# A new step order in the last mixing stage and a step table for the recurrence, in a two-block layer kernel

## The reference

```python
def rwkv7_mixer(...):                  # 16 heads of 64
    ...
    def step(state, inp):
        r_t, w_t, k_t, v_t, kk_t, a_t = inp
        sk = jnp.einsum('bhvk,bhk->bhv', state, kk_t)
        state = state * w_t[:, :, None, :] - sk[..., None] * (kk_t * a_t)[:, :, None, :] + v_t[..., None] * k_t[:, :, None, :]
        return state, jnp.einsum('bhvk,bhk->bhv', state, r_t)
    ...
    y = head_norm(y, LNX_EPS) * lnx_g + lnx_b
    bonus = jnp.sum(rh * kh * r_k, axis=-1, keepdims=True) * vh
    out = jnp.einsum('bsf,fd->bsd', (y + bonus) * jax.nn.silu(g), w_out)

def hgrn2_mixer(u, w_in, lb, out_gain, w_out):   # 8 heads of 128
    proj = u @ w_in
    q, fl, inp, g = jnp.split(proj, ...)
    log_f = jnp.logaddexp(jnp.log(lbf), jnp.log1p(-lbf) + jax.nn.log_sigmoid(fl))
    k = -jnp.expm1(log_f)
    ...  # chunk by chunk, b = cumsum(log_f)
        scores = jnp.einsum('bhtd,bhsd,bhtsd->bhts', qb, kb, decay)   # decay = exp(b_t - b_s), causal
        o = scores @ ib + jnp.einsum('bhtd,bhdv->bhtv', qb * jnp.exp(b), state)
        state = jnp.exp(b_last)[..., None] * state + jnp.einsum('bhsd,bhsv->bhdv', kb * jnp.exp(b_last - b), ib)
    o = o * lax.rsqrt(jnp.mean(o * o, axis=-1, keepdims=True) + EPS) * out_gain
    return (o * jax.nn.silu(g)) @ w_out
```

## Time and profile before

| | |
|---|---|
| median of 3 runs | 4136.17 us (4132.33 to 4144.88) |
| profiled execution | 4131.08 us, span of the core 4129.2 us |
| TensorE / its weight load | busy 90% / 73% of the span |
| VectorE / ScalarE | 49% / 40% |
| mean granted clock of TensorE | 0.919 |
| the recurrence's loop | about 1324 to 1980 us of the span |
| the last mixing stage | about 3270 to 3908 us of the span |

### The profile page before, as it was taken

The page is one execution under the profiler, slowest core; times in us unless marked ns, Lnnn a source line. Parts: engine busy times, 40 slices in busy tenths (PEclk is TensorE's granted clock), DMA queues, the critical chain, the costliest instruction groups (busy, mean ns, idle before and its releaser), DMA issues. The chain is left out here.

```text
span 4129.2 us, 48226 instructions
## 1 busy us (share of the span) xinstructions
PE 3724.6 (90%) x18866; PEld 3028.2 (73%) x18866; DVE 2018.7 (49%) x3934; ACT 1667.9 (40%) x3108; POOL 108.1 (3%) x120
## 2 busy tenths in 40 slices
PE   6999789989985999999797999999789999998799
PEld 5888458768873777777675777777677787877686
DVE  3144342453325667675435455555545455555542
ACT  3222461444422333433225344444432565655430
POOL 0011220000000000000000000000000000000000
PEclk9999899989995777788899999999889999999799
DMA  3332312122221211211411111010122211110221
GB/s 126 117 130 100 135 52 86 50 74 92 93 88 48 55 42 42 52 49 34 163 41 47 37 29 32 27 32 26 42 92 77 77 36 36 37 36 11 98 91 41
DMA packets 219705, 265.61 MB, mean 64 GB/s; under 512 B 62684, under 2 KB 142676, under 8 KB 218456
## 3 DMA queue, kind: packets, MB, share of 16 engines
q1 hardware_dynamic: 219480, 262.53, 19.6%
HBM read 191.95 MB, written 70.52 MB: 64 GB/s over the span
## 5 line engine op out<-in xcount | busy, mean ns | idle before, releaser
L320 PE MATMUL bank<-wh,XH 128*128 128x512 f32 x1344 | 553.3, 412 | 38.2 <-DVE wl L304 19.2
L320 PE MATMUL bank<-wh,XL 128*128 128x512 f32 x1344 | 528.3, 393 | 0.0
L320 PE MATMUL bank<-wl,XH 128*128 128x512 f32 x1344 | 528.3, 393 | 0.0
L2402 PE MATMUL bank<-XH,wh 128*128 128x512 f32 x1040 | 427.1, 411 | 32.1 <-DVE wl L2391 19.8
L2402 PE MATMUL bank<-XH,wl 128*128 128x512 f32 x1040 | 411.6, 396 | 0.0
L2402 PE MATMUL bank<-XL,wh 128*128 128x512 f32 x1040 | 410.3, 395 | 0.0
L320 PEld LDWEIGHTS bank<-wh,XH 128*128 128x128 f32 x1344 | 255.7, 190 | 101.8 <-issue 37.9
L320 PEld LDWEIGHTS bank<-wh,XL 128*128 128x128 f32 x1344 | 255.9, 190 | 60.2 <-issue 10.0
L320 PEld LDWEIGHTS bank<-wl,XH 128*128 128x128 f32 x1344 | 255.3, 190 | 55.2
L320 PE MATMUL bank<-XH,wh 128*128 128x512 f32 x704 | 278.3, 395 | 5.5 <-DVE XL L1512 5.5
L304 DVE TENSOR_TENSOR wl<-raw,wh 128x1024 fp32r<-128x1024 f32 x128 | 156.8, 1239 | 255.3 <-ACT wh L295 254.0
(11 more groups left out here) (406 smaller groups left out, 7187.7 us busy)
## 6 DMA issues: line engine op xcount, KB each, us to landing
sc_zt<-stage SPq DMA_DIRECT2D x88, 256.0 KB, 2.0
raw<-in_att_w_in SPq DMA_DIRECT2D x33, 512.0 KB, 4.2
raw<-in_even_w_in SPq DMA_DIRECT2D x32, 512.0 KB, 5.1
raw<-in_odd_w_in SPq DMA_DIRECT2D x32, 512.0 KB, 4.4
raw<-in_rec_w_in SPq DMA_DIRECT2D x32, 512.0 KB, 4.0
sc_h<-H SPq DMA_DIRECT2D x24, 512.0 KB, 2.6
sc_z<-stage SPq DMA_DIRECT2D x40, 256.0 KB, 2.1
z<-sc_z SPq DMA_DIRECT2D x8, 1024.0 KB, 5.5
```

What stands on the lines that cost most here:

```text
L320: done = e.matmul(out, lhsT, rhs, start=k == 0 and j == 0, stop=k == NK - 1 and j == 2)
L2402: done = e.matmul(bank[:, :], x[:, k, :], y[:, k, ts], start=k == 0 and j == 0, stop=k == NK - 1 and j == 2)
```

## The change

In `hgrn_order` the younger head's part is put before the older head's in each step, and VectorE's gate product becomes an event of its own (`gate`) one step after its tile, sorted to the end of that step. In `rwkv_order` the hand-written branches become the table `PLACED`, indexed by 3n + hop. Read against the old branches it places the same events at the same hops, except for two: the solver rows per hop are 4, 2, 3 (the last four in hop 15) in place of 3, 3, 3 (the last one in hop 16), and `gates` stands in hop 6, behind `pack` 1 and `load` of hop 5, in place of ahead of them. The attention stage is the same in both.

```diff
+PLACED = {
+    0: ((1, 'rh'), (1, 'alike', 1), (-1, 'tail', 1, 0)),
+    1: ((-1, 'tail', 1, 1),),
+    2: ((1, 'alike', 2), (1, 'rkr'), (-1, 'tail', 1, 2)),
+    3: ((1, 'alike', 3),),
+    4: ((1, 'pack', 0), (-1, 'tail', 1, 3)),
+    5: ((-1, 'tail', 1, 4), (-1, 'tail', 1, 5), (1, 'pack', 1), (1, 'bonus'), (2, 'load')),
+    6: ((1, 'solve', 4), (0, 'gates')),
+    7: ((1, 'solve', 2),),
+    8: ((2, 'lora', 0), (1, 'solve', 3)),
+    9: ((1, 'solve', 4),),
+    10: ((1, 'solve', 2),),
+    11: ((2, 'lora', 1), (2, 'scan'), (1, 'solve', 3), (0, 'tail', 0, 0)),
+    12: ((1, 'solve', 4),),
+    13: ((0, 'tail', 0, 1), (1, 'solve', 2)),
+    14: ((2, 'norm'), (0, 'tail', 0, 2), (1, 'solve', 3)),
+    15: ((1, 'solve', 4),),
+    16: ((0, 'tail', 0, 3),),
+    17: ((1, 'unpack'), (2, 'spread'), (2, 'centre')),
+    18: ((2, 'unit'),),
+    19: ((2, 'key'), (2, 'exps')),
+    20: ((0, 'tail', 0, 4),),
+    21: ((2, 'be'), (2, 'al')),
+    22: ((2, 'ka'), (0, 'tail', 0, 5)),
+    23: ((2, 'values'), (2, 'alike', 0)),
+}
...
-        some(p + 1, *[("solve", s) for s in solved(n, 0)])
...
-        elif n == 1:
-            if p:
-                order += [("tail", p - 1, 1, 4), ("tail", p - 1, 1, 5), ("gates", p)]
-            some(p + 1, ("pack", 1), "bonus")
-            some(p + 2, "load")
...
+            for q, what, *rest in PLACED[3 * n + j]:
+                if what == "solve":
+                    solve(p + q, rest[0])
+                elif not (what == "gates" and p == 0):
+                    some(p + q, (what, *rest))
...
@@ -2890,18 +2863,22 @@
     for t in range(11 * 7 + 22):
         h, s = min(t // 11, 7), t - 11 * min(t // 11, 7)
+        if s < 22:
+            put(t, "part", h, s)
         if h:
             put(t, "part", h - 1, s + 11)
-        if s < 22:
-            put(t, "part", h, s)
...
             if s == at:
                 tile(t, x, name, half)
+                if name == "g":
+                    put(t + 1, "gate", x, half)
...
+    for t in steps:
+        steps[t].sort(key=lambda x: x[0] == "gate")
...
-            elif what == "tile" and rest[0] == "g":
-                g = self.half(self.buf["g"][x], rest[1])
-                e.wait_ge(*self.copied.at(h, "g", rest[1]))
-                e.tensor_tensor(g, c.banks[self.mms[h, "g", rest[1]]][:, :], g, ALU.mult).then_inc(*self.gated.up(h, rest[1]))
+            elif what == "gate":
+                g = self.half(self.buf["g"][x], rest[0])
+                e.wait_ge(*self.copied.at(h, "g", rest[0]))
+                e.tensor_tensor(g, c.banks[self.mms[h, "g", rest[0]]][:, :], g, ALU.mult).then_inc(*self.gated.up(h, rest[0]))
```

More of the change, by code:

```diff
@@ L1615, in rwkv_order, with solve @@
     steps = [(p, n) for p in range(8) for n in range(NS)]
+    row = {}
     def some(q, *names):
-        if q < 8:
+        if 0 <= q < 8:
             order.extend((x[0], q, *x[1:]) if isinstance(x, tuple) else (x, q) for x in names)
+    def solve(q, rows):
+        for _ in range(rows):
+            some(q, ("solve", row.setdefault(q, 0)))
+            row[q] += 1
     some(0, "load", "values", "gates", ("lora", 0), ("lora", 1), "scan", "norm", "spread", "centre", "unit", "key", "exps", "be", "al")
@@ L1627, in rwkv_order @@
         some(1, *ahead.get(s, []))
-        some(0, ("solve", s))
+        solve(0, 1)
     some(0, "unpack")
@@ L1636, in rwkv_order @@
         group = groups[u // 2 + 1] if u < 62 else None
[L1637 to L1645, removed]
-            if p:
-                order.append(("tail", p - 1, 1, 0))
-        elif n == 1:
[L1649 to L1653, removed]
@@ L1703, in rwkv_order @@
-        some(p + 1, *[("solve", s) for s in solved(n, 2)])
+        for j, part in enumerate("ruy"):
+            order.append(("chain", p, n, part))
+            if after and part != "y":
+                order.append(("tokens" if part == "r" else "scores", *after))
+            level = {1: "X", 2: "G", 3: "Y", 4: "F"}.get(3 * (n % 2) + j)
+            if group and level:
+                order.append(("level", *group, level))
+            for q, what, *rest in PLACED[3 * n + j]:
[3 more added lines that the diff above has]
+                    some(p + q, (what, *rest))
@@ L1704, in rwkv_order @@
     order += [("tail", 7, 1, part) for part in range(6)]
     return order
-def solved(n, part):
-    at = 3 * (3 * (n - 2) + part)
-    return range(at, min(at + 3, NSUB)) if 2 <= n <= 5 else ()
 HALVES = (slice(0, 512), slice(512, 1024))
@@ L3105, in ac @@
                 e.activation(c.XH[:, h, :], self.back_row(h), ACT.Copy).then_inc(*self.high.up(h, 0))
-            else:
+            elif what == "part":
                 if h == 0 and rest[0] == 0:
```

## The result

The changed kernel takes 4039.5 us at the median of four runs (4033.9 to 4055.6), the kernel before 4140.5 in its four runs beside it (4132.3 to 4156.9): a ratio of 0.9758, 95% interval 0.9715 to 0.98. It is faster, as forecast, but by 101 us at the medians (97 from the 4136.2 that the forecast started from) where 61 were forecast; 4039.5 lies under the low end of the range, 4052. The profiled execution has a span of 4040.5 us against 4129.2. Of the 88.7 us between them, 37.8 lie in the recurrence of layer 2 (first products of chain r, first to last, 643.2 to 605.5 us) and 51.8 in all that follows it; its start is 0.9 us later.

What follows compares the result with a forecast made beforehand. TensorE was taken as the bound, losing time to waits for VectorE and lower clock. The last mixing stage's 48 us plus the recurrence's 13 gave 61: profiled 4070, median 4075 us, range 4052 to 4104.

Steps and rivals of the forecast that it cites:

- The last mixing stage: Stage repeated per head: the new order removes TensorE's 3.44 and 0.94 us waits and slow-clock products; 48 us saved.
- rival (1): Last mixing stage: the norm's chain replaces the gap, TensorE waits 1.8 us before the o transposes; 4099 us, chance 0.10.
- rival (4): Last mixing stage: late normed and gated outputs stall TensorE, paying back all 61 us or more; 4150 at 18 us, chance 0.02.
- (5): Last mixing stage: order changes nothing because the older head's state chain is the bound; 4123 us, chance 0.04.
- the last head's logarithm: Last head of the mixing stage: starting the logarithm before the key copy shortens the 4.59 us wait's chain by about 2 us.
- The landing of pn: Recurrence: with the gate load behind it, pn lands in 4.6 us, shortening chunk 3's waits; 12 us saved.
- the 0.5 that was the sign: Recurrence: TensorE's waits for the state at chunk 3 should fall under 0.5 us, except the last.
- Rival (2): Recurrence: pn no faster, as the store ahead and loads behind share DMA engines; only the stage gains; 4087 us, chance 0.06.
- The rows' new spread: Recurrence: solver rows 4, 2, 3 bring no state earlier; earlier unpacking after the last row is worth 1 us in all.
- The recurrence's clock: Recurrence: half clock in steps 3 counted as no gain; the six pairs together may move 10 us either way.
- Rival (3): Recurrence: the clock also recovers once its longest waits go, another 12 us; 4063 us, chance 0.08.
- The offset: Whole kernel: the median of runs, 4136.2 us, lies 5 us above the profiled execution; carried from 4070 to 4075.

Runs made afterwards that it cites:

- gate_only: Kernel before with only the last mixing stage's gate products a step later, old order of heads: 4114.8 us, 0.9942.
- pn_first: Kernel before with only the gate load moved behind pn and the next pair's loads, solver rows still 3, 3, 3: 4098.8 us, 0.9913.
- kr_first: Changed kernel with the next pair's loads k and r (1 MB) moved ahead of pn: 4093.9 us, 0.9885 to the kernel before.
- rows_only: Kernel before with only the solver rows 4, 2, 3 and the last row a hop earlier: 4133.5 us, 1.0001.
- stage_only: Kernel before with only the last mixing stage's new order, recurrence unchanged: 4087.1 us, 0.9881.
- swap_only: Kernel before with only the younger head's part put first, gate products left at their tiles: 4094.6 us, 0.9888.
- rows_ahead: Changed kernel with hop 11's three solver rows ahead of the second decay product and scan: 4039.8 us, 0.9771 to the kernel before.
- pack_early: Changed kernel with hop 11's solver rows first and pn's pack ahead of hop 5's two stores: 4040.5 us, 0.9778 to the kernel before.
- after_twice: Changed kernel with the 512-column lora products ahead of chunk 3 issued twice in six pairs: 4045.3 us, 0.9791 to the kernel before.
- norm_twice: Changed kernel with the 2-column norm products ahead of chunk 5's wait issued twice in six pairs: 4062.3 us, 0.9817 to the kernel before.
- norm_wide: Changed kernel with two extra 512-column products a pair ahead of chunk 5's wait, in six pairs: 4055.2 us, 0.9789 to the kernel before.
- lora_twice: Kernel before with the two 512-column products ahead of chunk 3's wait issued twice in six pairs: 4117.0 us, 0.9952.
- lora_narrow: Kernel before with eight extra 2-column products a pair ahead of chunk 3's wait: 4145.3 us, 1.001.

## Why the prediction was right and where it failed

**The last mixing stage: right, and a little low.** The signs that were asked for came: no wait for level 6, levels 6 and 7 in 3.65 us, and heads of 66.6 us, a little under the 67.2 forecast and the 67 to 68 named. The 0.5 us per head held back for hand-overs weren't needed. 51.8 us against 48. A wait where rival (1) put one comes only without the younger head's lead, and for the gate (gate_only, 1.66 us); rival (4)'s and (5)'s didn't show. The 2 us expected from the last head's logarithm were not seen as a shorter wait: 4.60 us stand there as 4.59 did.

**The landing of pn: right.** 4.7 us (4.6 taken), the waits of chunk 3 and with them the steps 2 shorter by 10.9 us (12 forecast), and pn_first shows that it is the gate load's place that does it. Two of the waits, 0.63 and 0.68 us, stay above the 0.5 that was the sign, and the new ones at chunk 4 weren't foreseen. Rival (2) is out: the loads behind pn did not cost it, as kr_first's opposite shows. The rows' new spread is worth nothing by itself (rows_only), as forecast.

**The recurrence's clock: the step that failed.** The prediction said of the half clock in the steps 3 that the first pair had it "which had no wait, so I count none of it", and kept 10 us either way. So the term of the clock stood at nothing in the sum. It measured 22.0 us in the steps 3 of pairs 1 to 5; the recurrence gained 37.8 us for 13, of which 4.8 are luck, pair 0's step 3. Rival (3) had the direction, at 12 us and a chance of 0.08. The ground for leaving it out was bad: pair 0 was one draw. In the four traces with the recurrence's code of before, its step 3 is 13.4, 8.6, 13.0 and 8.6 us, in the two of the changed kernel 8.6 and 13.4; in all thirteen traces with no work added ahead of it, it is 13.0 to 13.5 us in six and 8.6 to 9.2 in seven. In pairs 1 to 5 the picture isn't chance: with the gate load, or k and r, ahead of pn, all 30 of these steps in six kernels (before, stage_only, rows_only, swap_only, gate_only, kr_first) are 12.2 us or more; in the two traces of the changed kernel all ten are 9.2 or less. In all eight traces with the gate load behind pn and nothing put ahead of it (those two, pn_first, rows_ahead, pack_early, after_twice, norm_twice, norm_wide), 33 of 40 are (28 of 35 without after_twice, which has added work just ahead of them). One draw was read against a regular row of five, and the price is now read from the traces: 14.0 less 9.2 is 4.8 us a pair.

**The offset** of 5 us from the profiled execution to the median was carried over; in the changed kernel the median lies 2.8 us below the profiled time. With the stage's 3.8, the recurrence's 24.8 and this 7.8, less the 0.9 of the later start, the 35.5 us of the miss are accounted for.

**Shown and open.** Shown: an earlier pn gives most of the steps 3 their full clock (pn_first in part, the changed kernel in full), a later pn takes it (kr_first); filling the wait with 512-column products makes the kernel faster in spite of more work (lora_twice), filling it with 2-column products doesn't (lora_narrow). So it isn't the idle time alone, which was my theory until norm_twice. That the steps 3 carry most of the gain is read from the changed kernel's two traces; pn_first's own trace, 29 us above its median, can't confirm it. Open: what sets the half clock of the recurrence as a whole. pack_early, rows_ahead and norm_wide each removed waits or half clock in one step and found it in another, and the rows of pack_early show a fall after work that went without one elsewhere. All this rests on one profiled execution a kernel. Neither kind nor idle time, as read from a step, forecasts the sum. Why pn_first has two half-clocked steps 3 left isn't known; of the kernels that have the rows' spread as well, the changed one has none in ten and rows_ahead two in five. No version tried beats the changed kernel.

## What to carry to other kernels

Where a wait is followed by a stretch at the lower clock in pair after pair, price both, the wait and the slower stretch, before asking for a mechanism; a single case that goes the other way is worth a small chance, not a zero. Put the load that the critical chain waits for ahead of large loads that are wanted later in the same queue: moving 512 KB gave 36 to 42 us here, by the changed kernel's trace most of them through the clock. Once the waits are gone, take a further saving of waits in such a stage at less than its face value.

## What the runs showed of the hardware that was not expected

- More work made a kernel faster: some 11 us of extra 512-column products in a wait took 20 us off (a ratio of 0.9952, 0.9928 to 0.9975).
- The same wait filled with 2-column products took nothing off; in the pair shown the granted clock fell at 1438.2 us, as TensorE went without a pause from them to the products behind.
- Removing nearly all waits for pn and for the state (21.0 to 1.9 and 18.0 to 5.2 us) left the time unchanged, with 22 to 35 us more at half clock.
- The same code ran the same step (step 3 of pair 0) in 8.6 us in one execution and in 13.4 in another: 8.6 and 13.4 in the changed kernel, and 13.4, 8.6, 13.0 and 8.6 in the four kernels with the old recurrence.
- A 2-column float32 product runs as two passes, each with its own load of the weights, and a pass costs 0.21 us at half clock (6.83 us for 32) and 0.115 at full (1.84 for 16). In norm_twice's stretch of them, 1628.9 to 1635.7 us, the weight load was busy for all of the 6.80 us.
